# Two-block transformer on one core: scores, value product and sum of squares of the long heads issued inside weight tiles, and the weight split put ahead of the maxima

## The reference, cut to what matters

```python
s = jnp.einsum('bqhid,bkhid->bhiqk', qb.astype(jnp.float32) * ATTN_SCALE, k_all.astype(jnp.float32))
p = jax.nn.softmax(s, axis=-1)
a = p[:, :, 0] - lam * p[:, :, 1]
return jnp.einsum('bhqk,bkhe->bqhe', a.astype(v_all.dtype), v_all)
...
of = o.astype(jnp.float32)
y = of * lax.rsqrt(jnp.mean(jnp.square(of), axis=-1, keepdims=True) + RMS_EPS) * g * (1.0 - lam_init)
```

## Time and profile before

| | |
|---|---|
| median of 3 runs | 3728.88 us |
| lowest and highest | 3725.71 and 3730.09 us |
| span of the profiled execution | 3719.5 us |
| PE busy | 3467.2 us (93%) |
| DVE busy | 2288.1 us (62%) |
| ACT busy | 1303.7 us (35%) |
| share of PE in the chain that ended last | 72% |
| share of DVE in it | 10% |

### The profile page before, as it was taken

How to read it: one execution, slowest core, us unless ns; L and a number is a source line. 1 busy time by engine, 2 the same in 40 slices (tenths; PEclk the granted TensorE clock), 3 DMA queues, 4 the chain that set the end, 5 groups by cost and what they waited for, 6 DMA issues and landing times.

```text
span 3719.5 us, 48605 instructions
## 1 busy us (share of the span) xinstructions
PE 3467.2 (93%) x16800; PEld 2732.9 (73%) x16800; DVE 2288.1 (62%) x2909; ACT 1303.7 (35%) x1730; POOL 209.9 (6%) x396
## 2 busy tenths in 40 slices
PE   8699999899999999999799999999997998898996
PEld 2299989678777777878588777767785777687784
DVE  6455565886767764656655566665655888554433
ACT  0145544432334343225522334342326222344323
POOL 1000000000000000110000000000110000000000
PEclk9799999999999999998899999999998999999998
DMA  9844445445223222654554222221652222221231
GB/s 379 267 169 168 166 157 218 143 176 189 105 85 111 99 84 81 234 195 152 187 192 161 105 95 107 104 83 71 217 201 91 80 90 85 80 79 62 103 115 65
DMA packets 95158, 516.21 MB, mean 139 GB/s; under 512 B 11536, under 2 KB 11568, under 8 KB 55760
## 3 DMA queue, kind: packets, MB, share of 16 engines
q1 hardware_dynamic: 51328, 343.95, 25.4%
q0 software_dynamic: 43728, 170.91, 13.3%
HBM read 492.80 MB, written 22.02 MB: 138 GB/s over the span
## 4 chain that ended last, share of the span: by engine, by line
PE 72%; DVE 10%; issue 6%; DVEq 4%; DMA 4%; ACT 3%; ACTq 1%; POOL 0%; SPq 0%; POOLq 0%; PEldq 0%
PE acc L946 20%; PE acc L947 19%; PE acc L948 19%; DVE xy L1739 5%; PE S L1007 3%; PE pv L1041 2%; DVEq L1738 2%; PE S L1136 2%; DVE w_lo L1274 1%; PE misc L1118 1%; PE S L1015 1%; DMA bias_d<-evt 1%; PE S L1009 1%; DMA xy<-in_wm 1%; DVE gates L1321 1%
## 5 line engine op out<-in xcount | busy, mean ns | idle before, releaser
L946 PE MATMUL acc<-h_hi,w_hi 128*128 128x512 f32 (+1 forms) x4736 | 1747.3, 369 | 142.5 <-DVE h_lo L1280 67.6
L947 PE MATMUL acc<-h_lo,w_hi 128*128 128x512 f32 (+1 forms) x4736 | 1713.4, 362 | 0.0
L948 PE MATMUL acc<-h_hi,w_lo 128*128 128x512 f32 (+1 forms) x4736 | 1711.8, 361 | 0.0
L946 PEld LDWEIGHTS acc<-h_hi,w_hi 128*128 128x128 f32 x4736 | 908.5, 192 | 337.4 <-issue 126.2
L948 PEld LDWEIGHTS acc<-h_hi,w_lo 128*128 128x128 f32 x4736 | 909.4, 192 | 135.3
L947 PEld LDWEIGHTS acc<-h_lo,w_hi 128*128 128x128 f32 x4736 | 910.5, 192 | 132.0 <-issue 6.3
L1274 DVE TENSOR_TENSOR w_lo<-raw,w_hi 128x2048 fp32r<-128x2048 f32 x296 | 677.0, 2288 | 270.9 <-ACT w_hi L540 266.0
L540 ACT ACTIVATE w_hi<-raw 128x2048 fp32r<-128x2048 f32 x296 | 564.7, 1908 | 6.9 <-DVEq L1265 6.2
L540 ACT ACTIVATE ev<-acc 128x512 f32<-128x512 f32 (+1 forms) x210 | 110.8, 532 | 1255.9 <-PE acc L948 1222.7
L1321 DVE SCALAR_TENSOR_TENSOR gates<-gates,csil 128x512 f32<-128x512 f32 x568 | 412.2, 750 | 82.8 <-DMA gates<-in_wm 48.1
L1423 DVE TENSOR_REDUCE small<-S 128x2 f32<-128x1536 f32 (+1 forms) x80 | 123.4, 1543 | 309.7 <-PE S L1009 304.4
(11 more groups left out here) (199 smaller groups left out, 2160.2 us busy)
## 6 DMA issues: line engine op xcount, KB each, us to landing
raw<-in_w SPq DMA_DIRECT2D x296, 1024.0 KB, 4.8
gates<-in_wm POOLq DMA_DIRECT2D x216, 512.0 KB, 4.4
xy<-in_wm SPq DMA_DIRECT2D x32, 1024.0 KB, 10.0
x_d<-xy POOLq DMA_DIRECT2D x2, 4096.0 KB, 14.0
vtok<-in_wm POOLq DMA_DIRECT2D x8, 512.0 KB, 7.2
qb<-x_d POOLq DMA_DIRECT2D x16, 256.0 KB, 3.1
kb<-x_d POOLq DMA_DIRECT2D x16, 256.0 KB, 3.8
out_y<-xy POOLq DMA_DIRECT2D x4, 1024.0 KB, 4.1
```

Source lines behind the costliest of these rows:

```text
L946: mm(o, w_hi[:, w], h_hi[:, x], start=n == 0, stop=False)
L947: mm(o, w_hi[:, w], h_lo[:, x], start=False, stop=False)
L948: last = mm(o, w_lo[:, w], h_hi[:, x], start=False, stop=n == len(ks) - 1)
```

## The change

The context pass keeps its order, in functions of its own (`ctx_step`). For passes a and b:

- PE: scores p of a step are issued inside weight tile p, as `beside`, after nine of its matmuls; before, they stood between the transposes p - 1 and weight tile p. The transposes p stay after weight tile p.
- The value product of a step, the transposes of its values and the first scores go into weight tile 0 of the next step (`first`), the sum of squares into weight tile 1 (`second`), after its scores. Only step 8 keeps its own value product and sum of squares at its end. The steps 2 and 3 are written out, and PE's loop runs over steps 4 to 7.
- ACT: the squares of `pv` and the copy of the values go to the start of the next step, after `hi` and a wait for `qk_ready`, since the squares are written to `t1`, which the rotation uses. The square root goes from tile 0 to tile 1.
- DVE: `lo` is put ahead of the maxima in every tile. `mean_square` and `head_norm` go from tile 0 to tile 1, where the first part of `mod_tiles` is too.

SP's and POOL's streams are not edited. POOL's load of the next values from the context waits for `pv_done`, and stands behind the loads of its own step and ahead of the modulation weights of the next.

```diff
+                def step(i, proj=True, attn=True, norm=True, norm2=True, chunk=0, half=0):
+
+                    def first():
+
+                        if norm:
+                            values(i - 1)
+                        pe.wait_ge(acc_free, shown(acc_free, a_at(phase, i, -2) + 1))
+                        if norm2:
+                            pe.wait_ge(var_ready, shown(var_ready, At(h0 - 2, 1, i)))
+                        pe.wait_ge(vt_evac, shown(vt_evac, At(VT0[c] - 1, 1, i)))
+                        if phase in CHUNK0:
+                            pe.wait_ge(mod_out, shown(mod_out, chunk_at(phase, chunk)))
+                        value_transposes()
+                        scores(i, 0)
+
+                    def second():
+                        scores(i, 1)
+                        if norm:
+                            pe.wait_ge(vt_evac, shown(vt_evac, At(VT0[c], 1, i)))
+                            mean_squares(i - 1, t1)
+
+                    beside = (first, second, lambda: scores(i, 2), lambda: scores(i, 3))
+                    for p in range(4):
+                        at, n = (phase, i) if proj else (c + "pool", 0)
+                        weight_tile(j_at(at, n, p), a_at(at, n, p), T, H_AT[c + ".h"], beside=beside[p] if attn else None)
...
+                        if attn:
+                            transposes(i, p)
+                    if not proj:
+                        values(i)
+                        pe.wait_ge(var_ready, shown(var_ready, At(h0 - 1, 1, i)))
+                        mean_squares(i, last_osq)
```

ACT's step of passes a and b:

```diff
+                        hi(j_at(phase, i, p) + 1 if proj else j_at(c + "pool", 0, p + 1))
+                        if attn and p == 0:
+                            if norm:
+                                act.wait_ge(qk_ready, shown(qk_ready, At(h0, 1, i)))
+                                squared(i - 1, t1)
+                            value_evac(i - 1)
+                        if attn:
+                            exps(i, p)
+                        if norm and p == 1:
+                            root(i)
```

DVE's:

```diff
+                        lo(j_at(phase, i, p) + 1 if proj else j_at(c + "pool", 0, p + 1))
+                        if attn:
+                            maxima(i, p)
+                        if norm and p == 1:
+                            mean_square(i)
+                        if attn:
+                            difference(i, p)
+                        if norm and p == 1:
+                            head_norm(i)
                         if proj and phase in CHUNK0 and p in (1, 2):
                             mod_tiles(phase, chunk, (4 * half + 2 * p - 2, 4 * half + 2 * p - 1))
```

More of the change, by code:

```diff
@@ L611, in root, with exps @@
                     f(t2[:, 0:T], t2[:, 0:T], ACT.Sqrt).then_inc(sd_done, 1)
-                def step(i, proj=True, attn=True, norm=True):
+                def exps(i, p):
+                    n = At(N0[c] - QT + p, QT, i)
+                    act.wait_ge(nb_ready, shown(nb_ready, n + 1))
+                    act.wait_ge(t_done, shown(t_done, n))
+                    for m in range(2):
+                        e = f(maps[m][:, 0:NK], S[:, 1024 * m:1024 * m + NK], ACT.Exp,
+                              bias=small[:, m:m + 1], accum_out=small[:, 2 + m:3 + m])
+                    e.then_inc(exp_done, 1)
@@ new lines, in heads @@
+                act.wait_ge(dve_phase, shown(dve_phase, after(c + "conv")))
+                if c == "c":
+                    ctx_step(0, attn=False, norm=False)
+                    ctx_step(1, norm=False)
+                    loop(act, 2, N_HEADS, ctx_step)
+                    act.wait_ge(qk_ready, shown(qk_ready, h0 + N_HEADS))
+                    act.wait_ge(vt_done, shown(vt_done, VT0[c] + N_HEADS))
+                    act.wait_ge(gate_used, shown(gate_used, h0 + N_HEADS))
+                    ctx_step(N_HEADS, proj=False)
+                else:
+                    step(0, attn=False, norm=False)
+                    step(1, norm=False)
+                    loop(act, 2, N_HEADS, step)
+                    step(N_HEADS, proj=False)
@@ L1016, in transposes, with values, value_transposes, mean_squares @@
                     last.then_inc(t_done, 1)
-                def step(i, proj=True, attn=True, norm=True, chunk=0, half=0):
+                def values(i):
+                    pe.wait_ge(at_evac, shown(at_evac, At(N0[c], QT, i)))
+                    pe.wait_ge(vt_evac, shown(vt_evac, At(VT0[c], 1, i)))
+                    pe.wait_ge(y_done, shown(y_done, At(h0 - 1, 1, i)))
+                    if ctx_keys:
+                        pe.wait_ge(v_ld, shown(v_ld, At(16 * (h0 - 8), 16, i)))
+                    for k in range(NK // P):
+                        last = mm(pv[:, 0:T], vtok[:, P * k:P * (k + 1)], a_t[:, k * T:(k + 1) * T],
+                                  start=k == 0, stop=k == NK // P - 1)
+                    last.then_inc(pv_done, 1)
+                def value_transposes():
+                    for t in range(LT):
+                        last = nc.tensor.transpose(misc[:, P * t:P * (t + 1)], ev[2][:, P * t:P * (t + 1)], ident[:])
+                    last.then_inc(vt_done, 1)
+                def mean_squares(i, osq):
+                    pe.wait_ge(osq_done, shown(osq_done, At(h0, 1, i)))
+                    mm(misc[:, 0:T], ones[:], osq[:, 0:T], start=True, stop=True).then_inc(ms_done, 1)
+                def ctx_step(i, proj=True, attn=True, norm=True):
                     for p in range(4):
@@ L1034, in step @@
                     if attn:
-                        pe.wait_ge(at_evac, shown(at_evac, At(N0[c], QT, i)))
-                        pe.wait_ge(vt_evac, shown(vt_evac, At(VT0[c], 1, i)))
-                        pe.wait_ge(y_done, shown(y_done, At(h0 - 1, 1, i)))
-                        if ctx_keys:
-                            pe.wait_ge(v_ld, shown(v_ld, At(16 * (h0 - 8), 16, i)))
-                        for k in range(NK // P):
-                            last = mm(pv[:, 0:T], vtok[:, P * k:P * (k + 1)], a_t[:, k * T:(k + 1) * T],
-                                      start=k == 0, stop=k == NK // P - 1)
-                        last.then_inc(pv_done, 1)
+                        values(i)
                     if proj:
@@ L1064, in two_steps @@
                     step(i * 2 + 1, chunk=i, half=1)
-                step(0, attn=False, norm=False)
-                step(1, norm=False, half=1)
-                loop(pe, 1, N_HEADS // 2, two_steps)
-                step(N_HEADS, proj=False)
+                if c == "c":
+                    ctx_step(0, attn=False, norm=False)
+                    ctx_step(1, norm=False)
+                    loop(pe, 2, N_HEADS, ctx_step)
+                    ctx_step(N_HEADS, proj=False)
+                    return
+                step(0, attn=False)
+                step(1, norm=False, norm2=False, half=1)
+                step(2, norm2=False, chunk=1)
+                step(3, chunk=1, half=1)
+                loop(pe, 2, N_HEADS // 2, two_steps)
+                step(N_HEADS, proj=False, chunk=N_HEADS // 2)
             def mix(c, g):
```

204 lines of the change are left out of this document (112 added, 92 removed).

## The result

| | median of the runs | lowest and highest |
|---|---|---|
| before | 3729.49 us (4 runs) | 3725.71 and 3732.84 |
| changed | 3694.61 us (4 runs) | 3690.59 and 3705.00 |

The ratio is 0.9915, with a 95% interval of 0.9898 to 0.9931: the changed kernel is faster, by 32 us by the ratio and by 35 by the medians. The forecast was 3690.8, with a range of 3668 to 3711. The profiled execution of the changed kernel has a span of 3695.9 us and a device time of 3697.44.

What follows compares the result with a forecast made beforehand. PE was taken to bound the kernel, with waits hidden in its busy time. 46.1 + 17.6 - 6.4 - 19.2 = 38.1 us gained, off the median 3728.9: 3690.8 us, range 3668 to 3711.

Steps and rivals of the forecast that it cites:

- What bounds the kernel: Passes a and b: PE sets the time, with 0.96 us of waiting hidden in busy time 24 times a pass.
- (1): Scores inside weight tiles 1 to 3 no longer wait for ACT's copy: 46.1 us gained for both passes.
- (2): Value product inside tile 0 no longer waits for ACT's copy, save in step 8: 17.6 us gained for both passes.
- (5): ACT's squares and value copy, POOL's loads and SP's queue come in time at no cost; context pass under 1 us.
- (3): Entering and leaving attention tiles once more, 0.1 us a switch: 6.4 us lost, between 0 and 19.
- (4): Transposes wait for DVE's difference, mostly in tile 2 of pass a: 19.2 us lost together.
- The distance of 9.4 us between span and median: Median 3728.88 against profiled span 3719.5; the distance is taken as fixed, giving a span of 3681.4.
- DVE keeps pace: Rival: pass a's stalls stay near zero, gain 57 us, 3672; chance 0.15.
- Switches at 0.3: Rival: score weights are not loaded ahead at the switches, 13 us less gain, 3704; chance 0.13.
- Late in both passes: Rival: DVE's difference is late, tiles 1 to 3 each wait 1 us, about 3729; chance 0.07.
- slower: Rival: the split is held up by ACT's rounding and SP's load; at 2 us a tile, 3768; chance 0.07.
- The signs: PE's timeline: scores 1.5 to 1.7 us, stalls before transposes 2; step pairs 1.5 us shorter in pass a, 7.2 in b.

Runs made afterwards that it cites:

- the second experiment: Changed kernel with the first part of the modulation products moved from tile 1 to tile 0 (products in tiles 0 and 2): 3665.59 us, ratio 0.9831.
- the second profile: Changed kernel run again without an edit, beside the kernel before on the same chip: 3694.16 us, ratio 0.9905.
- the fourth experiment: Changed kernel with scores 1 to 3 back behind the transposes, only the end of the step moved: 3722.04 us, ratio 0.9978.

## Why the prediction held, step by step

**What bounds the kernel:** right. A PE that is shown busy 98% of a pass had 23 us of waiting in each. The difference of two starts showed it, the idle time did not.

**(1) Scores inside the tiles, 46.1:** right, 45.8 measured with that part alone.

**(2) The value product, 17.6:** right. Pass b gained 8.5 by it alone, and (1) and (2) together gave 32.0 and 32.3 where 31.8 a pass were forecast. These sums hold two small errors that offset each other: step end by step end the second experiment gained 1.09 and 1.72 us where 1.01 and 1.59 were forecast, and step 8 gained less than its share of (1), as said under (5). The nine matmuls ahead of the product cover ACT's copy, as the unbroken rows of tile 0 show.

**(3) The switches, 6.4 lost:** mis-sized. A middle tile without a stall takes 13.28 to 13.29 us in the changed kernel. It took 14.26 before, and less the 0.96 of term (1) that is 13.30. A switch costs 0.00, the lower end of the bounds, as in pooling. The step that failed is the choice of 0.1 between the row in pooling and the weight load. Neither the entry into the 64-row scores nor the way back costs any time. By the Trainium skill (TensorE: Matmul & The Clock Gate, The mechanism) a weight load overlaps running matmuls only where the row group differs. The trace disagrees: held at the switches alone, that rule would have cost 0.19 each. The same section also says that a load can be pulled ahead of running matmuls when it targets the background weight buffer, and with that the trace agrees.

**(4) The stalls, 19.2 lost:** right in place, cause and size. Each link:

| | predicted | measured |
|---|---|---|
| transposes 2 of pass a, even step | 2.27 | 2.40 to 2.41 |
| transposes 2 of pass a, odd step | 2.95 | 3.17 |
| transposes 3 of pass a, even step | 0.80 | 0.70 twice, none once |
| transposes 2 of pass b, even / odd | 0 / 0.37 | about 0.2 / 0.52 to 0.53 |
| the waits named, in sum | 19.2 | 19.7 |
| length of tile 0 | 19.1 | 18.89 to 18.98 |

So laying DVE's links end to end, with durations from the trace of before, gives such a stall to 0.2 us. What the sum lacked is what an idle PE costs after it: 0.4 to 1.7 us more in the tile behind most of the longer stalls, 3.8 us of pass a in one profile and 6.8 in the other. The second experiment, which has no stalls, gives the whole of it: its heads gain 64.3 us, and the changed kernel's 36.9. Of the 27.4 between them 19.7 are the waits; the other 7.7 come with them, 3.8 of these as slow matmuls in pass a and the rest as tenths in many tiles. In the second profile they are 12.2. Against the 6.4 of (3) that nearly cancels, and that is luck: with the switches rightly at nothing, the sum would have been 44.5 us, 7.6 above the 36.9 that the heads gained. By pass the errors don't cancel: a kept 7.5 where 10.5 were forecast, and b gave 29.4 where 27.6 were. The profile before had clock 1.00 in both passes, with idle times of up to 1.52 us in them, so it gave no price; "the clock has nothing to give back" was true, but it had something to lose.

**The distance of 9.4 us between span and median:** this step failed. Where a run has both numbers, the device time is 1.5 to 2.8 us above the span, mostly 1.6 (3697.44 and 3695.9 here). If that held for before too, its profiled execution was simply some 8 us faster than the median of its kernel. To take the sum off the median was sound all the same, as the result shows; the span of 3681.4 was not, and 3695.9 came.

**The rivals.** "DVE keeps pace" (3672) is false of the changed kernel: its idle time lay where the products were not. It is what the kernel does once these are moved, and then with 3665.6, since switches are free. "Switches at 0.3" is false. "Late in both passes" and "slower" rest on a chain of 11.6 in a tile of 13.4 us, and the twice-done split shows that the margin is real: with 2.3 us more in that chain, 64 us are lost. No link was longer than in the trace of before, save one in step 8 (below), so neither came in the changed kernel.

**(5) At nothing:** right, but for one wait in step 8. No wait for `qk_ready`, keys or values shows on PE in passes a and b. The context pass, with its own functions now, takes as long as before (220.7 to 221.1 us in all kernels). That one wait comes in both passes. The prediction said that it would be wrong if half 0 of the scores still waited for ACT's copy, and in tile 2 of step 8 it does:

```profile
1407.03 1.33 PE L1051 MATMUL S<-kb,qb 64*128 64x512 f32 x3
...
1409.14 0.50 PE L990 MATMUL acc<-h_hi,w_hi 128*128 128x512 f32 x1
```

The scores take 2.11 us instead of 1.50 and the tile 13.92 instead of 13.29. The transposes start at 1404.21, but ACT first loads a function table (1405.01 to 1406.29) and copies the gate, and its copy of the transposes ends at 1407.60. Before, the same tile was only 0.29 longer than its neighbours. This costs 0.6 us a pass, and no list of waits names it. At the end of step 8 the value product waits as before (2.4 us in two waits), as said. The sum of squares waits there too, but nearly as much as before (`PE misc L1081 <- ACT work L540: 2.1, 3, 0.8`; it was 1.8 in three waits).

**The signs.** The stalls came where they were said to, at the lengths in the table. A pair of an even and an odd step got 7.6 us shorter in pass b (7.2 forecast). In pass a the three pairs got 1.1, 0.0 and 0.0 us shorter where 1.5 was forecast: there the slow matmuls took it.

## What to carry to other kernels

A wait that stands between two matmuls of one group is not idle time in a profile: compare the start-to-start time of a piece of work in two places, one where it waits and one where it cannot, before believing a busy share of 98%. When work moves into the tiles of the bounding engine, lay out the chain on the engine that feeds it link by link. Put what others wait for (the maxima) ahead of what can hide beside them (the split), and put filler such as the modulation products into the longest tile: here each of these two alone brought 26 to 29 us on top of the 35 of the change. The longest tile is also one without the head's norm here, and the runs do not separate the two reasons. Two edits that remove the same stall do not add up, so try each alone first.

## What the runs showed of the hardware

- Behind an idle time on PE the granted clock was sometimes lower for four to five microseconds, with means of 0.57 to 0.68, that is mostly the lower of the two levels (1.2 GHz); matmuls then take up to 0.63 instead of 0.39 us. It added up to 1.7 us to the tile, half as much again as the stall of 3.17. The price is smaller where the slower engine would have been waited for anyway. With the products in tiles 0 and 2, which leaves no stall in it, the stretch of pass a (880 to 1370) had clock 1.00.
- It does not follow each time. The stretches behind the six stalls of 2.4 and 3.17 us in pass a of the changed kernel, in turn (columns as above):

```profile
1033.00:1037.00 4.00, 4.00 (x14) 2.77 (x14) 3.79 (x6) 2.61 (x2) 0.00 (x0) 0.59 0.00 0
1097.00:1101.00 4.00, 4.00 (x21) 2.90 (x23) 3.73 (x6) 2.62 (x2) 0.00 (x0) 1.00 0.01 4
1161.00:1165.00 4.00, 4.00 (x21) 2.88 (x23) 3.73 (x6) 2.61 (x2) 0.00 (x0) 1.00 0.02 4
1225.00:1229.00 4.00, 4.00 (x14) 3.48 (x15) 3.79 (x6) 2.48 (x2) 0.00 (x0) 0.59 0.03 12
1291.00:1295.00 4.00, 4.00 (x22) 2.54 (x21) 3.83 (x6) 2.61 (x2) 0.00 (x0) 1.00 0.00 0
1355.00:1359.00 4.00, 4.00 (x16) 3.07 (x14) 3.78 (x6) 2.61 (x2) 0.00 (x0) 0.63 0.04 16
```

  The clock fell behind three of the six; in the second profile of the same kernel behind all six (0.57 to 0.63). With the split done twice, it fell behind five of six stalls of only 1.86 to 1.89 us in pass a, and behind one of six (1.82 to 1.90 us) in pass b. Length alone doesn't decide it: the clock fell behind a wait of only 0.90 us with the scores alone inside the tiles (0.66 from 1227 to 1232, the value product taking 7.10 us where 5.41 is usual) and behind one of 1.15 us in the fourth experiment (0.66), and did not behind the longest, of 3.36 us. What tells the cases apart stays open.
- A group of matmuls put inside another's accumulation, with weights of 64 rows between weights of 128, costs its own time and no more (13.29 us against 13.30 worked out).
- A load of ACT's function tables takes 1.28 us; in a place where PE waits for ACT's next copy, it shows on PE (a tile of 15.95 us instead of 14.55 in pass b of the fourth experiment, 13.92 instead of 13.29 in the changed kernel).
